# Four edits at the starts of three stages of a two-block transformer kernel on one core: input products in step with the shift on ScalarE, a first chunk split on GpSimd, raw gates copied out, post norm sums on TensorE

## The chip, the core and the metric

The kernel runs on one core of one Trainium2 chip. The core has TensorE (PE, matrix products out of SBUF into eight PSUM banks), VectorE (DVE), ScalarE (ACT), GpSimd (POOL) and SyncE (SP, which issues the DMAs). Each engine runs its own list of instructions in order, and they meet by semaphores. The metric is the time of one execution on the device in microseconds; lower is better.

## The reference, cut to what matters

Two blocks follow each other on x of 512 tokens by 1024 features, all in float32. Of the first block:

```python
h = rms_norm(x, mix_pre_norm) * (1 + sc_m) + sh_m
proj = h @ w_in                      # cq, ckv, index keys, then the inputs of the RWKV group
...
x = x + g_m * rms_norm(mix, mix_post_norm)
hf = rms_norm(x, ffn_pre_norm) * (1 + sc_f) + sh_f
f = (silu(hf @ w_ffn_gate) * (hf @ w_ffn_up)) @ w_ffn_down
x = x + g_f * rms_norm(f, ffn_post_norm)
```

The second block begins with

```python
h = h + 0.5 * swiglu(rms_norm_2(h, norm_ffn[0, 0]), ffn_w_gate, ffn_w_up, ffn_w_down)
```

## The kernel before, in words

The activations stand transposed in SBUF: `x` and `h` are eight tiles of 128 features by 512 tokens. A product of float32 matrices is made of three products of rounded numbers: each operand is split into a high part (a rounding copy by ScalarE) and a low part (the operand less its high part, by VectorE), and TensorE adds high x high, high x low and low x high. Weights stream from HBM in chunks of 1 MB (eight rows of 128 by 256 columns) through a ring of four slots; `Split.high` and `Split.low` split each chunk into `wt_hi` and `wt_lo`, of which there are two each. Chunks are loaded by SyncE as soon as the chunk four before is split (`low_done`). The order of the instructions on each engine is the order in which the code is written; nothing reorders them.

Three stages are touched.

**inproj**, the input products (`in_proj_stage`, by way of `linear_part`). The first chunk, in_q, gives two output tiles, in_kv one, then twelve of in_rkv. Before, `normed_vector` makes each of the eight features in two instructions on VectorE, times gain and norm (L713, the norm's value standing in a bank) and plus the shift (L716). ScalarE copies the high part; the low part of even tiles is VectorE's (L720), of odd ones GpSimd's (L748). The chunk is split whole (L521, L536), and `product3` runs through the eight features for output tile 0, then again for tile 1. Between in_kv and in_rkv stands `ik_product`, the product of the index keys, a plain float32 product of `h` itself (L814): it is the first to need the tiles of `h`.

**ffn1** (`ffn_part` with `mix`). The stage begins with two norms at once (`MixNorm`): VectorE forms five small columns (`new_squares`, L435 to L443, 128x4 in `coef`), ScalarE takes the root, VectorE the inverse, and TensorE spreads both norms over banks 5 and 7 (L428). Then VectorE updates each tile k in three instructions (L458: h times coefficient and norm; L460: x plus h; L464: the next norm), and the low part is the fourth (L471). The first chunk is split in four quarters, by ScalarE (L548) and VectorE (L564), between these. `first_chunks` makes TensorE go through the features once, for the two gate tiles and, three features behind, the two up tiles.

**ffn2** (`ffn_part` with `post`), behind ffn1 in the same section. ffn1's output f lies in `h`. `PostNorm` needs its column sums of squares: six tiles are summed by GpSimd while ffn1 ends (into `acc`, named mcq in the trace), the last two are squared by ScalarE and added by VectorE (L299), and TensorE sums the one tile over its partitions (L308). Root, inverse and spread (L318, L322, L312) follow, then for each tile VectorE's two instructions of `update` (L328 into a bank, L330 from it into x) and the low part (L674); ScalarE makes the high part (L653) and the square (L654), and GpSimd adds the squares for the next norm (L740). That norm is applied late (`defer`): gates and ups are products of the un-normed features, and VectorE multiplies them by the inverse root `rs` (L691, L697, L703), gates before SiLU (L1271). A product into the gate banks 0 and 1 waits until the gates in them are scaled (`s_gate`).

## Time and profile before

| what | value |
| --- | --- |
| median of 3 runs | 2852.81 us (2852.09 to 2854.67) |
| the profiled execution | 2850.93 us |
| its span | 2849.1 us |
| TensorE busy | 2718.7 us, 95% of the span |
| VectorE busy | 1318.2 us, 46% |
| ScalarE busy | 845.7 us, 30% |
| GpSimd busy | 550.8 us, 19% |
| mean granted clock of TensorE | 0.975 |

The profile is one execution as the hardware recorded it. Its span runs from the first to the last instruction; the time of the execution is a little longer. Busy is the sum over an engine's instructions. The granted clock is a share of TensorE's full speed, 2.4 GHz, and has two levels, so 0.5 is 1.2 GHz. Names on the left of `<-` are written, those on the right read; `bank` is PSUM, all others are SBUF or, with `in_`, HBM.

### The profile page before, as it was taken

How to read it: one execution, taken by the hardware profiler on the slowest of the kernel's cores; microseconds unless marked ns; L12 is line 12 of the kernel's file. 1: busy time of each engine (PE TensorE's matmuls, PEld its weight loads, DVE VectorE, ACT ScalarE, POOL GpSimd, SP SyncE). 2: the span in 40 equal slices, each digit the busy share in tenths (PEclk: the TensorE clock that was granted, in tenths of full speed). 3: DMA queues.
4: the chain of work that ended last, by engine and by line, in shares of the span. 5: the costliest groups of instructions: out<-in, count | busy, mean ns of one | idle time of the engine just before them, and what ended most of it. 6: DMA issues, size and time to landing. Idle time of an engine off the chain costs nothing. (4 is left out here: it accounts for less than half of the span.)

```text
span 2849.1 us, 39056 instructions
## 1 busy us (share of the span) xinstructions
PE 2718.7 (95%) x16402; PEld 2167.3 (76%) x16402; DVE 1318.2 (46%) x1862; ACT 845.7 (30%) x1264; POOL 550.8 (19%) x379
## 2 busy tenths in 40 slices
PE   6989898989999899999989999999999999999998
PEld 4768764778888688887858888888888746788886
DVE  3464668553333633435455434353333556543433
ACT  3231235531212422123253212132222346421212
POOL 2000113412112230212301202123021100031202
PEclk8999989989999899999999999999999999999999
DMA  8250310123232223323203232233232230233221
GB/s 262 62 177 4 121 37 4 60 74 104 89 104 79 84 95 98 104 78 105 89 1 116 92 103 89 89 104 104 89 104 80 62 104 1 89 104 103 89 93 41
DMA packets 256943, 248.26 MB, mean 87 GB/s; under 512 B 25972, under 2 KB 252088, under 8 KB 256640
## 3 DMA queue, kind: packets, MB, share of 16 engines
q1 hardware_dynamic: 256562, 245.70, 27.6%
q8 instruction: 130, 2.13, 0.3%
q14 instruction: 45, 0.37, 0.0%
q10 hardware_dynamic: 206, 0.06, 0.0%
HBM read 241.52 MB, written 2.12 MB: 86 GB/s over the span
## 5 line engine op out<-in xcount | busy, mean ns | idle before, releaser
L536 DVE TENSOR_TENSOR dense_wt_lo<-ring,dense_wt_hi 128x2048 fp32r<-128x2048 f32 (+1 forms) x177 | 437.6, 2472 | 291.1 <-ACT dense_wt_hi L521 291.1
L521 ACT CAST dense_wt_hi<-ring 128x2048 fp32r<-128x2048 f32 (+1 forms) x177 | 328.1, 1854 | 764.6 <-PE bank L796 752.8
L1292 POOL TENSOR_TENSOR dense_act_hi<-dense_act,const 128x512 fp32r<-128x512 f32 x110 | 214.8, 1952 | 1326.7 <-DVE dense_act L1284 1326.7
L796 PE MATMUL bank<-feat_hi,dense_wt_hi 128*128 128x512 f32 x1344 | 416.0, 391 | 2.9 <-DVE dense_silu L1271 2.9
L796 PE MATMUL bank<-feat_lo,dense_wt_hi 128*128 128x512 f32 x1344 | 414.9, 390 | 0.0
L796 PE MATMUL bank<-feat_hi,dense_wt_lo 128*128 128x512 f32 x1344 | 414.8, 390 | 0.0
L796 PEld LDWEIGHTS bank<-feat_hi,dense_wt_hi 128*128 128x128 f32 x1344 | 253.0, 188 | 56.6 <-issue 4.3
L796 PEld LDWEIGHTS bank<-feat_lo,dense_wt_hi 128*128 128x128 f32 x1344 | 253.0, 188 | 52.7
L796 PEld LDWEIGHTS bank<-feat_hi,dense_wt_lo 128*128 128x128 f32 x1344 | 252.9, 188 | 52.6
L796 PE MATMUL bank<-dense_act_hi,dense_wt_hi 128*128 128x512 f32 x912 | 282.3, 391 | 6.4 <-DVE dense_act_lo L604 5.5
L796 PE MATMUL bank<-dense_act_hi,dense_wt_lo 128*128 128x512 f32 x912 | 281.5, 390 | 0.0
L796 PE MATMUL bank<-dense_act_lo,dense_wt_hi 128*128 128x512 f32 x912 | 281.4, 390 | 0.0
L796 PEld LDWEIGHTS bank<-dense_act_hi,dense_wt_hi 128*128 128x128 f32 x912 | 171.2, 188 | 44.1 <-DVE dense_wt_lo L601 5.9
L796 PEld LDWEIGHTS bank<-dense_act_lo,dense_wt_hi 128*128 128x128 f32 x912 | 171.5, 188 | 35.8
L796 PEld LDWEIGHTS bank<-dense_act_hi,dense_wt_lo 128*128 128x128 f32 x912 | 171.5, 188 | 35.7
L1284 DVE TENSOR_TENSOR dense_act<-dense_silu,bank 128x512 f32<-128x512 f32 x110 | 70.7, 684 | 259.7 <-PE bank L796 258.7
L1262 DVE SCALAR_TENSOR_TENSOR x<-bank,x 128x512 f32<-128x512 f32 x96 | 61.8, 686 | 234.2 <-PE bank L796 234.2
L1215 ACT ACTIVATE dense_silu<-dense_silu 128x512 f32<-128x512 f32 x88 | 54.1, 632 | 390.9 <-DVE dense_silu L1271 390.9
L1271 DVE TENSOR_TENSOR dense_silu<-bank,rs 128x512 f32<-128x512 f32 x88 | 56.7, 686 | 230.3 <-PE bank L796 229.7
L1294 POOL TENSOR_TENSOR dense_act_lo<-dense_act,dense_act_hi 128x512 fp32r<-128x512 f32 x110 | 150.6, 1369 | 16.5 <-issue 1.3
L272 POOL TENSOR_TENSOR h<-h 128x512 f32<-128x512 f32 x30 | 39.2, 1305 | 409.7 <-ACT h L257 408.6
L796 PE MATMUL bank<-last_feat_hi,dense_wt_hi 128*128 128x512 f32 x352 | 108.9, 390 | 0.0
(619 smaller groups left out, 3787.3 us busy)
## 6 DMA issues: line engine op xcount, KB each, us to landing
ring<-in_ffn_w_gate SPq DMA_DIRECT2D x44, 1024.0 KB, 5.3
ring<-in_ffn_w_up SPq DMA_DIRECT2D x44, 1024.0 KB, 5.3
ring<-in_ffn_w_down SPq DMA_DIRECT2D x32, 1024.0 KB, 5.1
ring<-in_ada_w SPq DMA_DIRECT2D x24, 1024.0 KB, 7.5
ring<-in_ffn_w_down SPq DMA_DIRECT2D x16, 768.0 KB, 4.4
...
```

The source lines that it names most:

```text
L272: K.nc.gpsimd.tensor_tensor(K.h[:, 0, :], K.h[:, 0, :], K.h[:, k, :], ALU.add)
L521: self.nc.scalar.copy(self.wh[:, n % 2, 0:words], K.ring[:, n % RING, 0:words]).then_inc(K.high_done, 1)
L536: self.nc.vector.tensor_tensor(self.wl[:, n % 2, 0:words], K.ring[:, n % RING, 0:words], self.wh[:, n % 2, 0:words].bitcast(F32), ALU.subt ...
L796: lasts[m] = pe.matmul(outs[m], a, b, start=n == 0 and p == 0, stop=end and p == 2)
L1215: nc.scalar.activation(g[:, m, :], g[:, m, :], ACT.Silu).then_inc(s_silu, 1)
L1262: v.scalar_tensor_tensor(to, bank, 0.5, to, ALU.mult, ALU.add).then_inc(s_free, 1)
L1271: v.tensor_tensor(g[:, m, :], K.bank[m][:, :], K.rs[:, :], ALU.mult).then_inc(s_gate, 1)
L1284: v.tensor_tensor(a[:, m, :], g[:, m, :], K.bank[2 + m][:, :], ALU.mult).then_inc(s_act, 1)
L1292: nc.gpsimd.tensor_tensor(ah[:, f, :], a[:, i % 2, :], K.k("ones")[:, 0:1].broadcast_to([P, T]), ALU.mult)
L1294: nc.gpsimd.tensor_tensor(al[:, f, :], a[:, i % 2, :], ah[:, f, :].bitcast(F32), ALU.subtract).then_inc(s_al, 1)
```

## The change

Four edits, each at one of the three stages.

1. *inproj.* It gets a `NormedSource` and takes the path that three other stages had (`source_scalar`, `source_vector`): ScalarE and VectorE split the first chunk in quarters between the features, and TensorE makes the two tiles of in_q in step, six products for each feature. A feature is made by one instruction of VectorE (gain and norm); ScalarE adds the shift as it makes the high part, VectorE as it makes the low one, for all eight tiles. Since `ik_product` needs the whole `h`, GpSimd adds the shift in place once the low part of that tile is out, and TensorE waits for all eight before `ik_product`. That GpSimd makes no low parts any more is part of it.
2. *ffn1.* The four quarters of the first chunk are subtracted by GpSimd (`mix_pool`) in place of VectorE, and VectorE waits for them before it splits chunk 1.
3. *ffn2, the gates.* ScalarE copies the two raw gate tiles of the first chunk from their banks into the SiLU tile; the product of chunk 2 waits for these copies in place of the scaled gates, and VectorE scales the copies.
4. *ffn2, the post norm.* The two last squares are summed by TensorE into the same columns as the tile of sums, so that VectorE's two additions go. And in VectorE's loop the low part of tile k-1 now stands between the two instructions of tile k.

```diff
-    def add(self, dve):
-        v = self.K.nc.vector
-        for m in range(2):
-            dve.wait_ge(self.s_sq, m + 1)
-            ins = v.tensor_tensor(self.acc, self.acc, self.sq[m], ALU.add)
-            if m == 0:
-                dve.drain()
-        ins.then_inc(self.s_add, 1)
-
-    def sums(self, pe):
+    def sums(self, pe, prev):
+
         K = self.K
-        pe.wait_ge(self.s_add, 1)
-        for b in range(TB):
-            last = pe.matmul(K.bank[6][:, b:b + 1], self.acc[:, b * P:(b + 1) * P], K.k("ones")[:, 0:1], start=True, stop=True)
+        pe.wait_ge(prev.s_acc, 1)
+        pe.wait_ge(prev.done[0], prev.done[1] - 2)
+        for m, x in enumerate([self.acc] + list(self.sq)):
+            if m:
+                pe.wait_ge(self.s_sq, m)
+            for b in range(TB):
+                last = pe.matmul(K.bank[4][:, b:b + 1], x[:, b * P:(b + 1) * P], K.k("ones")[:, 0:1], start=m == b == 0, stop=m == 2 and b == TB - 1)
         last.then_inc(self.s_sum, 1)
         pe.wait_ge(self.s_inv, 1)
...
-    def update(self, dve, k):
-        K, v = self.K, self.K.nc.vector
+    def scale(self, dve, k):
+        K = self.K
         if k == 0:
             dve.wait_ge(self.s_spread, 1)
-        v.scalar_tensor_tensor(K.bank[4 + 2 * (k % 2)][:, :], K.h[:, k, :], self.coef(k), K.bank[5][:, :], ALU.mult, ALU.mult)
+        K.nc.vector.scalar_tensor_tensor(K.bank[4 + 2 * (k % 2)][:, :], K.h[:, k, :], self.coef(k), K.bank[5][:, :], ALU.mult, ALU.mult)
         dve.drain()
-        v.tensor_tensor(K.x[:, k, :], K.bank[4 + 2 * (k % 2)][:, :], K.x[:, k, :], ALU.add).then_inc(self.s_x, 1)
+
+    def add(self, k):
+        K = self.K
+        K.nc.vector.tensor_tensor(K.x[:, k, :], K.bank[4 + 2 * (k % 2)][:, :], K.x[:, k, :], ALU.add).then_inc(self.s_x, 1)
...
-        K, v = self.K, self.nc.vector
+    def mix_pool(self, pool):
+        K = self.K
         n = self.pieces
-        self.mix.new_squares(dve)
         for j in range(4):
             part = slice(2 * j * WC, 2 * (j + 1) * WC)
-            dve.wait_ge(self.s_wh, j + 1)
-            v.tensor_tensor(self.wl[:, n % 2, part], K.ring[:, n % RING, part], self.wh[:, n % 2, part].bitcast(F32),
-                            ALU.subtract).then_inc(self.s_wl, 1)
-            if j == 1:
-                self.mix.inverse(dve)
-        dve.drain().then_inc(K.low_done, 1)
+            pool.wait_ge(self.s_wh, j + 1)
+            self.nc.gpsimd.tensor_tensor(self.wl[:, n % 2, part], K.ring[:, n % RING, part], self.wh[:, n % 2, part].bitcast(F32),
+                                         ALU.subtract).then_inc(self.s_wl, 1)
+        pool.drain().then_inc(K.low_done, 1)
+
+    def mix_vector(self, dve, name):
+        K = self.K
+        self.mix.new_squares(dve)
+        self.mix.inverse(dve)
         for k in range(KD + 1):
             if k < KD:
                 self.mix.update(dve, k)
@@ -573,6 +568,7 @@
                 dve.wait_ge(self.s_hh, k)
                 self.mix.low(self.hl[:, k - 1, :], self.hh[:, k - 1, :], k - 1).then_inc(self.s_hl, 1)
             if k == 2:
+                dve.wait_ge(K.low_done, K.plan.segments[name]["split0"] + 1)
                 self.low(dve, name, 1)
...
-            if source.ready(k):
-                act.wait_ge(*source.ready(k))
-            c(self.hh[:, k, :], source.tile(k)).then_inc(self.s_hh, 1)
+            source.high(act, k, self.hh[:, k, :]).then_inc(self.s_hh, 1)
         act.drain().then_inc(K.high_done, 1)
 
     def source_vector(self, dve):
         K, source, v = self.K, self.source, self.nc.vector
         n = self.pieces
+        source.make(dve, source.order[0])
         for at, k in enumerate(source.order):
             if at % 2 == 0:
                 part = slice(k * WC, (k + 2) * WC)
                 dve.wait_ge(self.s_wh, at // 2 + 1)
                 v.tensor_tensor(self.wl[:, n % 2, part], K.ring[:, n % RING, part], self.wh[:, n % 2, part].bitcast(F32),
                                 ALU.subtract).then_inc(self.s_wl, 1)
+            if at + 1 < KD:
+                source.make(dve, source.order[at + 1])
             dve.wait_ge(self.s_hh, at + 1)
-            v.tensor_tensor(self.hl[:, k, :], source.tile(k), self.hh[:, k, :].bitcast(F32), ALU.subtract).then_inc(self.s_hl, 1)
+            source.low(k, self.hl[:, k, :], self.hh[:, k, :].bitcast(F32)).then_inc(self.s_hl, 1)
         dve.drain().then_inc(K.low_done, 1)
...
             for k in range(KD + 1):
                 if k < KD:
-                    self.post.update(dve, k)
+                    self.post.scale(dve, k)
                 if k:
                     dve.wait_ge(self.s_hh, k)
                     v.scalar_tensor_tensor(self.hl[:, k - 1, :], K.x[:, k - 1, :], self.defer(k - 1), self.hh[:, k - 1, :].bitcast(F32),
                                            ALU.mult, ALU.subtract).then_inc(self.s_hl2 if k % 2 == 0 else self.s_hl, 1)
+                if k < KD:
+                    self.post.add(k)
...
-    def normed_vector(self, dve):
-
-        K, v = self.K, self.nc.vector
-        gain, shift = self.norm
-        if self.rstd:
-            dve.wait_ge(self.rstd.s_out, 1)
-        for k in range(KD):
-            ins = v.scalar_tensor_tensor(K.h[:, k, :], K.x[:, k, :], gain(k), self.value, ALU.mult, ALU.mult)
...
-                ins = v.tensor_scalar(K.h[:, k, :], K.h[:, k, :], shift(k), None, ALU.add)
...
     def features_vector(self, dve, first_low, name=None):
-        self.first_low = first_low
-        if self.norm:
-            return self.normed_vector(dve)
         if self.defer:
             if not self.prev:
                 first_low(dve)
@@ -741,11 +703,9 @@
                 if k < KD - 1:
                     pool.drain()
             ins.then_inc(self.s_add, 1)
-        if not self.norm:
-            return
-        for k in range(1, KD, 2):
-            pool.wait_ge(self.s_hh, k + 1)
-            self.nc.gpsimd.tensor_tensor(self.hl[:, k, :], K.h[:, k, :], self.hh[:, k, :].bitcast(F32), ALU.subtract).then_inc(self.s_hl2, 1)
+        if self.mix:
+            self.mix_pool(pool)
...
-                    if i >= 2:
+                    if post and c == 2:
+                        pe.wait_ge(s_raw, 2)
+                    elif i >= 2:
...
                 if c == 0:
+                    for m in range(2 if post else 0):
+                        act.wait_ge(K.tiles_done, plan.tile(name, c, m))
+                        nc.scalar.copy(g[:, m, :], K.bank[m][:, :]).then_inc(s_raw, 1)
...
-                        dve.wait_ge(K.tiles_done, plan.tile(name, c, m))
-                        v.tensor_tensor(g[:, m, :], K.bank[m][:, :], K.rs[:, :], ALU.mult).then_inc(s_gate, 1)
+                        if post and c == 0:
+                            dve.wait_ge(s_raw, m + 1)
+                        else:
+                            dve.wait_ge(K.tiles_done, plan.tile(name, c, m))
+                        v.tensor_tensor(g[:, m, :], g[:, m, :] if post and c == 0 else K.bank[m][:, :], K.rs[:, :], ALU.mult).then_inc(s_gate, 1)
...
-            if source and j == 0:
+            if source and (seg, j) == chunks[0][:2]:
...
+    def high(self, act, k, dst):
+        if self.ready(k):
+            act.wait_ge(*self.ready(k))
+        return self.nc.scalar.copy(dst, self.tile(k))
+
+    def low(self, k, dst, high):
+        return self.nc.vector.tensor_tensor(dst, self.tile(k), high, ALU.subtract)
+
+
+class NormedSource:
+
+    order, front, shift = range(KD), None, 0
+
+    def __init__(self, K, gain, bias, value):
+        self.K, self.gain, self.bias, self.value = K, gain, bias, value
+
+    def begin(self, st):
+        self.s_h, self.s_whole = st.sems("normed", "shifted")
+
+    def make(self, dve, k):
+        K = self.K
+        K.nc.vector.scalar_tensor_tensor(K.h[:, k, :], K.x[:, k, :], self.gain(k), self.value, ALU.mult, ALU.mult).then_inc(self.s_h, 1)
+
+    def high(self, act, k, dst):
+        act.wait_ge(self.s_h, k + 1)
+        return self.K.nc.scalar.activation(dst, self.K.h[:, k, :], ACT.Identity, bias=self.bias(k))
+
+    def low(self, k, dst, high):
+        return self.K.nc.vector.scalar_tensor_tensor(dst, self.K.h[:, k, :], self.bias(k), high, ALU.add, ALU.subtract)
+
+    def whole(self, pool, s_hl):
+        K = self.K
+        for k in range(KD):
+            pool.wait_ge(s_hl, k + 1)
+            K.nc.gpsimd.tensor_scalar(K.h[:, k, :], K.h[:, k, :], self.bias(k), None, ALU.add).then_inc(self.s_whole, 1)
...
         pe.wait_ge(box["wik_in"], 16)
+        pe.wait_ge(source.s_whole, KD)
         product(pe, K.bank[6][0:72, :], [(box["wik"][:, k, :], K.h[:, k, :]) for k in range(KD)]).then_inc(box["ik_pe"], 1)
...
-    def causal(pool):
+    def on_pool(pool):
+        source.whole(pool, box["split"].s_hl)
         pool.wait_ge(box["scored"], 1)
...
+    source = NormedSource(K, *norm, K.norm_value)
     linear_stage(K, "inproj", tiles, banks=6, scalar=lambda t: False,
```

The places where the order moves, as lists of instructions. GpSimd in inproj, from the start of the stage (`branch`) to its end, before and after:

```order
L886 UNCONDITIONAL_BRANCH
L748 TENSOR_TENSOR inproj__feat_lo<-h,inproj__feat_hi 128x512 [waits inproj__feat_high] x4
L1728 ISA [waits inproj__scored]
L1728 AFFINE_SELECT y<-y 128x128
L865 UNCONDITIONAL_BRANCH
```

```order
L846 UNCONDITIONAL_BRANCH
L1497 ISA
L1497 TENSOR_SCALAR h<-h,mod 128x512 [waits inproj__feat_low_even] x8
L1738 AFFINE_SELECT y<-y 128x128 [waits inproj__scored]
L825 UNCONDITIONAL_BRANCH
```

Four subtractions that waited for high parts give way to eight additions in place that wait for low parts; the selection on the scores stays behind them.

VectorE in inproj, from its first instruction in the stage, before and after, both up to feature 3:

```order
L713 SCALAR_TENSOR_TENSOR h<-x,coef,bank 128x512
L716 TENSOR_SCALAR h<-h,mod 128x512
L713 SCALAR_TENSOR_TENSOR h<-x,coef,bank 128x512
L716 TENSOR_SCALAR h<-h,mod 128x512
L720 TENSOR_TENSOR inproj__feat_lo<-h,inproj__feat_hi 128x512 [waits inproj__feat_high]
L536 TENSOR_TENSOR inproj_wt_lo<-ring,inproj_wt_hi 128x2048 [waits high_done]
L713 SCALAR_TENSOR_TENSOR h<-x,coef,bank 128x512
L716 TENSOR_SCALAR h<-h,mod 128x512
L713 SCALAR_TENSOR_TENSOR h<-x,coef,bank 128x512
L716 TENSOR_SCALAR h<-h,mod 128x512
```

```order
L1484 SCALAR_TENSOR_TENSOR h<-x,coef,bank 128x512
L596 TENSOR_TENSOR inproj_wt_lo<-ring,inproj_wt_hi 128x512 [waits inproj__first_high]
L1484 SCALAR_TENSOR_TENSOR h<-x,coef,bank 128x512
L1491 SCALAR_TENSOR_TENSOR inproj__feat_lo<-h,mod,inproj__feat_hi 128x512 [waits inproj__feat_high]
L1484 SCALAR_TENSOR_TENSOR h<-x,coef,bank 128x512
L1491 SCALAR_TENSOR_TENSOR inproj__feat_lo<-h,mod,inproj__feat_hi 128x512 [waits inproj__feat_high]
L596 TENSOR_TENSOR inproj_wt_lo<-ring,inproj_wt_hi 128x512 [waits inproj__first_high]
L1484 SCALAR_TENSOR_TENSOR h<-x,coef,bank 128x512
L1491 SCALAR_TENSOR_TENSOR inproj__feat_lo<-h,mod,inproj__feat_hi 128x512 [waits inproj__feat_high]
```

The shift (L716) is gone from VectorE, the split of the chunk stands in quarters between the features, and each feature is made one ahead of the low half before it.

VectorE at the start of ffn1, the columns of the two norms and the first update, before and after:

```order
L435 TENSOR_TENSOR coef<-bank,coef 128x4
L437 SCALAR_TENSOR_TENSOR coef<-bank,coef 128x4
L439 TENSOR_TENSOR coef<-coef 128x4
L441 TENSOR_TENSOR coef<-coef 128x4
L443 TENSOR_SCALAR coef<-coef 128x4
L564 TENSOR_TENSOR dense_wt_lo<-ring,dense_wt_hi 128x512 x2
L452 RECIPROCAL coef<-coef 128x4
L564 TENSOR_TENSOR dense_wt_lo<-ring,dense_wt_hi 128x512 x2
L458 SCALAR_TENSOR_TENSOR h<-h,coef,bank 128x512
```

```order
L434 TENSOR_TENSOR coef<-bank,coef 128x4
L436 SCALAR_TENSOR_TENSOR coef<-bank,coef 128x4
L438 TENSOR_TENSOR coef<-coef 128x4
L440 TENSOR_TENSOR coef<-coef 128x4
L442 TENSOR_SCALAR coef<-coef 128x4
L451 RECIPROCAL coef<-coef 128x4
L457 SCALAR_TENSOR_TENSOR h<-h,coef,bank 128x512
L459 TENSOR_TENSOR x<-x,h 128x512
```

The four subtractions around the inverse (L452, now L451) are gone; GpSimd has them.

VectorE at the start of ffn2, from the inverse of the post norm, before and after:

```order
L322 RECIPROCAL ffn_post_col<-ffn_post_col 128x4
L536 TENSOR_TENSOR dense_wt_lo<-ring,dense_wt_hi 128x2048
L328 SCALAR_TENSOR_TENSOR bank<-h,coef,bank 128x512
L330 TENSOR_TENSOR x<-bank,x 128x512
L328 SCALAR_TENSOR_TENSOR bank<-h,coef,bank 128x512
L330 TENSOR_TENSOR x<-bank,x 128x512
L674 SCALAR_TENSOR_TENSOR feat_lo<-x,par,feat_hi 128x512
L328 SCALAR_TENSOR_TENSOR bank<-h,coef,bank 128x512
L330 TENSOR_TENSOR x<-bank,x 128x512
```

```order
L318 RECIPROCAL ffn_post_col<-ffn_post_col 128x4
L529 TENSOR_TENSOR dense_wt_lo<-ring,dense_wt_hi 128x2048
L324 SCALAR_TENSOR_TENSOR bank<-h,coef,bank 128x512
L329 TENSOR_TENSOR x<-bank,x 128x512
L324 SCALAR_TENSOR_TENSOR bank<-h,coef,bank 128x512
L657 SCALAR_TENSOR_TENSOR feat_lo<-x,par,feat_hi 128x512
L329 TENSOR_TENSOR x<-bank,x 128x512
L324 SCALAR_TENSOR_TENSOR bank<-h,coef,bank 128x512
L657 SCALAR_TENSOR_TENSOR feat_lo<-x,par,feat_hi 128x512
```

The low part of tile k-1 moved from behind to ahead of the addition of tile k.

ScalarE in ffn2, from the square of the last tile, before and after:

```order
L654 ACTIVATE h<-x 128x512
L521 CAST dense_wt_hi<-ring 128x2048
L697 ACTIVATE rs<-bank,const 128x512
L1215 ACT_TABLE_LOAD
L1215 ACTIVATE dense_silu<-dense_silu 128x512 x2
L521 CAST dense_wt_hi<-ring 128x2048
L1215 ACTIVATE dense_silu<-dense_silu 128x512 x2
```

```order
L637 ACTIVATE h<-x 128x512
L1167 COPY dense_silu<-bank 128x512 x2
L514 CAST dense_wt_hi<-ring 128x2048
L682 ACTIVATE rs<-bank,const 128x512
L1180 ACT_TABLE_LOAD
L1180 ACTIVATE dense_silu<-dense_silu 128x512 x2
L514 CAST dense_wt_hi<-ring 128x2048
L1180 ACTIVATE dense_silu<-dense_silu 128x512 x2
```

Two copies of banks into the SiLU tile now stand ahead of the cast of chunk 2 and of the root.

## Rows read from the trace of the kernel before

**Rows 1.** Waits of TensorE: us in all, times, longest.

```profile
PE bank L806 <- DVE feat_lo L471: 8.3, 2, 4.9
...
PE bank L806 <- DVE feat_lo L674: 4.6, 2, 3.8
```

**Rows 2.** Timeline, input products: start us, us, instruction [idle before, releaser].

```profile
43.99 0.75 DVE L713 SCALAR_TENSOR_TENSOR h<-x,coef,bank 128x512 f32<-128x512 f32 x1 [0.32 <-PEq L1027]
...
49.41 0.79 PE L780 MATMUL bank<-inproj__feat_hi,inproj_wt_hi 128*128 128x512 f32 x1 [6.19 <-DVE inproj_wt_lo L536]
...
73.01 7.03 PE L814 MATMUL bank<-h,y 128*72 128x512 f32 x16
```

**Rows 3.** Timeline, VectorE and GpSimd; two lines' kinds: least, median, longest ns.

```profile
47.06 2.29 DVE L536 TENSOR_TENSOR inproj_wt_lo<-ring,inproj_wt_hi 128x2048 fp32r<-128x2048 f32 x1
...
47.26 3.23 POOL L748 TENSOR_TENSOR inproj__feat_lo<-h,inproj__feat_hi 128x512 fp32r<-128x512 f32 x1 [12.49 <-ACT inproj__feat_hi L647]
...
963.79 1.28 POOL L740 TENSOR_TENSOR h<-h 128x512 f32<-128x512 f32 x1 [14.98 <-ACT h L654]
...
964.44 1.18 DVE L674 SCALAR_TENSOR_TENSOR feat_lo<-x,par,feat_hi 128x512 fp32r<-128x512 f32 x1
...
L674 DVE SCALAR_TENSOR_TENSOR feat_lo<-x,par,feat_hi x8: 743/749/1193, 962.4 to 977.1; 128x512 fp32r<-128x512 f32 x8
...
L2639 POOL TENSOR_SCALAR abin__acc<-abin__acc x4: 1491/2419/3592, 1349.2 to 1374.2; 128x512 f32<-128x512 f32 x4
```

**Rows 4.** Timeline, start of ffn1.

```profile
575.75 1.14 ACT L548 CAST dense_wt_hi<-ring 128x512 fp32r<-128x512 f32 x2 [2.11 <-PEq L865]
...
576.45 0.16 DVE L441 TENSOR_TENSOR coef<-coef 128x4 f32<-128x4 f32 x1
...
576.77 1.28 DVE L564 TENSOR_TENSOR dense_wt_lo<-ring,dense_wt_hi 128x512 fp32r<-128x512 f32 x2
...
576.89 0.30 ACT L448 ACTIVATE coef<-coef,const 128x4 f32<-128x4 f32 x1
...
578.20 2.07 PE L428 MATMUL bank<-const,coef 128*128 128x128 f32 x8 [0.40 <-DVE coef L452]
...
579.81 0.75 DVE L458 SCALAR_TENSOR_TENSOR h<-h,coef,bank 128x512 f32<-128x512 f32 x1 [0.49 <-issue]
...
585.20 1.19 PE L806 MATMUL bank<-feat_hi,dense_wt_hi 128*128 128x512 f32 x2 [4.93 <-DVE feat_lo L471]
```

**Rows 5.** Timeline, start of ffn2.

```profile
954.65 1.88 ACT L521 CAST dense_wt_hi<-ring 128x2048 fp32r<-128x2048 f32 x1
...
956.84 0.26 ACT L318 ACTIVATE ffn_post_col<-bank,const 128x4 f32<-128x4 f32 x1 [0.31 <-PE bank L308]
...
960.92 0.75 DVE L328 SCALAR_TENSOR_TENSOR bank<-h,coef,bank 128x512 f32<-128x512 f32 x1
...
970.31 0.73 PE L806 MATMUL bank<-feat_hi,dense_wt_hi 128*128 128x512 f32 x2 [0.84 <-DVE feat_lo L674]
...
974.81 0.74 DVE L328 SCALAR_TENSOR_TENSOR bank<-h,coef,bank 128x512 f32<-128x512 f32 x1
```

**Rows 6.** Timeline, ffn2 behind its first two chunks.

```profile
982.23 0.62 PE L806 MATMUL bank<-feat_hi,dense_wt_lo 128*128 128x512 f32 x2
...
982.68 0.62 PE L806 MATMUL bank<-feat_hi,dense_wt_hi 128*128 128x512 f32 x2
...
982.94 1.91 ACT L521 CAST dense_wt_hi<-ring 128x2048 fp32r<-128x2048 f32 x1 [5.33 <-PE bank L806]
...
987.18 3.35 DVE L703 RECIPROCAL rs<-rs 128x512 f32<-128x512 f32 x1
...
992.12 1.19 PE L796 MATMUL bank<-feat_hi,dense_wt_hi 128*128 128x512 f32 x2 [2.93 <-DVE dense_silu L1271]
```

**Rows 7.** Window: us, busy of five engines, clock, DMA; group of the page: busy, mean.

```profile
992.20:998.20 6.00, 6.00 (x15) 4.76 (x16) 5.12 (x5) 2.22 (x2) 3.86 (x2) 0.52 0.00 0
...
L1215 ACT ACTIVATE dense_silu<-dense_silu 128x512 f32<-128x512 f32 x88 | 54.1, 632 | 390.9 <-DVE dense_silu L1271 390.9
```

80 lines of the change are left out of this document (27 added, 53 removed).

## The prediction, made before the changed kernel had run

> **What bounds the kernel now.** I read the page first: TensorE is busy for 95% of the span (the table above), so an edit gains only where TensorE stands still or runs at the lower of its two clocks. The chain that ended last is no help here, being put down mostly to issue. The waits of TensorE and the timeline around them name the places, and the change works at four of them. TensorE stands 4.9 and 3.4 us (8.3 together) for `feat_lo` at the start of ffn1 and 4.6 us for `feat_lo` at the start of ffn2 [rows 1], 6.2 us before the input products [rows 2], and 2.9 us for `dense_silu` in ffn2 [rows 6]. In the input products TensorE starts at 49.41, 5.4 us after VectorE's first instruction, and reaches the product of the index keys at 73.01 [rows 2]. At both ffn starts it is VectorE that paces the first features [rows 4, 5]. Everywhere between, TensorE is dense, so I take a shift at one of these places as carried whole to the end.
>
> **A port that two edits meet.** Edits 1 and 2 both give GpSimd work while VectorE sets the pace, so I read how the two run together [rows 3]. GpSimd's subtraction that started at 47.26, just behind VectorE's 2.29 us one, took 3.23 us; its instruction at 963.79, with nothing ahead, 1.28. The other way round VectorE's `feat_lo` at 964.44, begun under that GpSimd instruction, took 1.18 us, where the least of its kind is 0.743. GpSimd's one kind of TENSOR_SCALAR took 1.49 us at the least and 3.59 at the most. So one engine waits for the other's whole instruction when both read SBUF with two tiles in play.
>
> The Trainium skill ("SBUF — State Buffer", "Who interferes with whom") says more: a VectorE instruction with two SBUF inputs contends with any GpSimd instruction that reads SBUF, and the first to issue keeps the pair to its end. The 3.23 and 1.18 agree; that VectorE waits for a GpSimd TENSOR_SCALAR no row here shows. By the page edit 1 gains next to nothing; without it, the 7 us that are worked out below. It speaks against edits 1 and 2.
>
> **Edit 1, input products.** *Without the port:* VectorE makes feature 0 at 43.99 (0.75 us, and the next instruction starts some 0.66 behind), splits a quarter of the chunk (0.64, half of the x2 of 1.28 [rows 4]), makes feature 1 and takes the low half of 0, so TensorE starts near 46.8, 2.6 us earlier. A feature then costs VectorE 0.66 + 0.66 + 0.64/2 = 1.64 us. TensorE's six products of it take 2.55 us at the lower clock (0.425 each, 14 in the 6.0 us of [rows 7]) and 1.36 at the higher (0.2265 each: two start 0.45 behind two [rows 6]). With some 16 products at the lower clock the two tiles end near 60.4 and in_kv's 24 products near 65.9, where before the key product started at 73.0: 7 us gained.
> *With the port:* GpSimd adds the shift to tile k once low k is out, eight times 1.49 us. Each falls under VectorE's making of the next feature, which reads a bank, and the next low half, with two SBUF inputs, waits for its end. Two features cost 0.64 (quarter) + 2 x (1.49 + 0.66) = 4.9 us, less the overlap of one instruction's end with the next; I step 4.7 to 5.1. Low 0 ends at 46.6, low 1 at 48.9, low 3 at 54.0, low 5 at 59.1, low 7 at 64.2. GpSimd's last addition then starts at once (64.3 to 65.8), ahead of VectorE's split of in_kv, half as wide as the 2.29 us one (1.4). in_kv's products run 67.3 to 72.8: 0.2 us gained. Of the ends I take 0.2, since the operations are those of [rows 3] but for one operand. ScalarE's shift and casts lie under VectorE. The ring's next load is issued some 15 us later (the first split is complete at 64.3, not 49.4), but its chunk is the fifth of the stage, a 5 us transfer with 30 us before it is cast: hidden.
>
> **Edit 2, GpSimd splits ffn1's first chunk.** It takes four subtractions of 0.64 us off VectorE, which hold the update of feature 0 to 579.81 [rows 4]. *Left alone* VectorE could update at 577.9, when the first spread (2.07 us from 575.75) is out; the second spread behind it ends at 579.9, where the step that needs it came 1.6 us after 579.81: 1.5 us gained. *With the port:* GpSimd's first quarter starts at 576.4, when the first of ScalarE's two casts is out, and the product of two `coef` columns at 576.45 has two SBUF inputs. It waits to 577.7. The next small instruction may wait for the second quarter, to 579.1; then come the root (0.30), the inverse, the second spread to 582.0, and the sum x+h under the third quarter. TensorE's first product starts at 586.1 in place of 585.20: 0.9 us lost. If the small instruction, with one input, doesn't wait, the same steps gain 0.25. I take 0.9 lost, since both waits are for whole instructions as in [rows 3]; bounds: 1.5 gained, 1.5 lost.
>
> **Edit 4 and the new order of the post norm, ffn2.** Two additions go from VectorE and 16 small products come to TensorE, most of them under ScalarE's squares. ScalarE's cast (954.65, 1.88 us) holds the root to 956.55; before, the root waited 0.31 us longer, to 956.84 [rows 5]: 0.3 us gained. Then VectorE's loop. Before, a feature's step comes every (974.81 - 960.92)/6 = 2.32 us [rows 5], of which about 2.1 are three instructions and the rest the port: GpSimd's sum of squares meets every second low half (0.743 against 1.19 [rows 3]). In the new order the low half comes before the addition, which reads a bank, and 0.6 us before the square that starts GpSimd; the two stop meeting, and a step takes about 2.15. Feature 1's step starts at 960.62, feature 4's at 967.07, and low 3, 0.83 behind it, is out at 968.7; TensorE waits for it until 970.31 now and is dense behind it. 1.6 us gained in all; at the least 0.3, the root alone, should the higher clock come later.
>
> **Edit 3, raw gates copied out.** Before, TensorE ends the first two chunks near 989.2 and waits for gates scaled by the inverse (3.35 us from 987.18) to 992.12 [rows 6]: 2.9 us. After that idle time the granted clock is 0.52 for 6.0 us, in which 14 products take 0.425 each instead of 0.2265 [rows 7]: 2.8 us. Now ScalarE copies the gates (2 x 0.63, as its activations of this size [rows 7]) before the cast of chunk 2, which started at 982.94. Counted with the 1.6 above: copies 981.3 to 982.6, cast (1.9) to 984.5, VectorE's split (2.29) to 986.8; TensorE ends at 987.6 and goes on at once, at the full clock. The inverse runs from 986.8, the activations come at 994.2, chunk 3's split at 997, and TensorE wants it at 998.5. Gained: 2.9 + 2.8 = 5.7 us. The cover is thin, 0.8 us at chunk 2 and 1.5 at chunk 3; if it goes, some 3 us are left.
>
> **The sum.** -0.2 + 0.9 - 1.6 - 5.7 = -6.6 us. The profiled execution took 2850.93 (span 2849.1 and 1.8 around it), so 2844.3; the median of the runs lies 1.9 above it. I say **2846 us**.
>
> **The rivals.**
> *The port doesn't bind in the input products* (the addition of a column isn't held, or doesn't hold VectorE): 7 us instead of 0.2, so 2839. For it: no row shows VectorE waiting for a TENSOR_SCALAR. Against: GpSimd's own was stretched to 3.59 [rows 3]. Chance 0.15.
> *The gates' cover is gone:* chunk 2's split comes late behind copies and cast, TensorE waits two us and the clock falls all the same. 5.7 shrinks to 2 or 3: 2849. Against: 0.8 us of slack. Chance 0.15.
> *Slower, GpSimd's additions are slow.* The key product waits for all eight, and each holds VectorE, so each us more of an addition's own time moves in_kv by 8. To lose the 6.4 us of the other terms and 0.2% more takes 12.1 us: an addition of 1.49 + 12.1/8 = 3.0 us or more. The stretched ones took up to 3.59, but 2.1 of that was VectorE's. At 3.3 us it is 2860. Chance 0.07.
> *As forecast:* 0.63, own range 2842 to 2849.
>
> **Range and chances.** 2838 to 2851 takes in the first two rivals and the bounds of edit 2, and leaves out the third. A measurement tells about 0.2%, 5.7 us, from no change: below 2847.1 is faster. Of the forecast's 0.63 I put 0.43 below that, 0.19 within and 0.01 above; the first rival is faster; of the second 0.01 is faster and 0.14 within. Faster 0.59, same 0.33, slower 0.08.
>
> **What would show it.** Input products: TensorE starts at 46.8, GpSimd has eight TENSOR_SCALARs on `h` of 1.5 us or stretched, VectorE low halves of up to 1.4 us, and the key product starts near 72.8. ffn1: a small `coef` row of over 1 us, TensorE's first product 0.9 us later against the stage's start. ffn2: steps of 2.15 us, no wait for `dense_silu`, granted clock 1.00 there. Wrong it would be if the key product starts near 66, if the clock stays low through the first two tiles, or if TensorE still stops behind ffn2's second chunk.

## The result and the profile after

| | before | after |
|---|---|---|
| median of the runs, us | 2853.02 (2852.09 to 2854.67, 4 runs) | 2836.01 (2835.05 to 2841.01, 4 runs) |
| ratio of after to before | | 0.9944, 95% interval 0.9932 to 0.9956 |
| profiled execution, us (its span) | 2850.93 (2849.1) | 2836.70 (2834.8) |

The change takes about 16 us off where 6.6 were forecast, and the median lies 2 us below the range. A second, later comparison of the same two kernels gave 0.9949 (0.9937 to 0.9961), which is 14.5 us.

The timeline of the input products after the change, the counterpart of [rows 2]:

```profile
43.13 0.75 DVE L1484 SCALAR_TENSOR_TENSOR h<-x,coef,bank 128x512 f32<-128x512 f32 x1 [0.32 <-PEq L987]
...
45.06 0.75 DVE L1491 SCALAR_TENSOR_TENSOR inproj__feat_lo<-h,mod,inproj__feat_hi 128x512 fp32r<-128x512 f32 x1
...
45.91 12.86 POOL L1497 TENSOR_SCALAR h<-h,mod 128x512 f32<-128x512 f32 x8 [11.78 <-DVE inproj__feat_lo L1491]
45.95 1.19 PE L756 MATMUL bank<-inproj__feat_hi,inproj_wt_hi 128*128 128x512 f32 x2 [3.60 <-DVE inproj__feat_lo L1491]
...
46.38 0.76 DVE L1491 SCALAR_TENSOR_TENSOR inproj__feat_lo<-h,mod,inproj__feat_hi 128x512 fp32r<-128x512 f32 x1
...
54.83 2.06 DVE L1491 SCALAR_TENSOR_TENSOR inproj__feat_lo<-h,mod,inproj__feat_hi 128x512 fp32r<-128x512 f32 x2
...
57.34 1.63 DVE L529 TENSOR_TENSOR inproj_wt_lo<-ring,inproj_wt_hi 128x1024 fp32r<-128x1024 f32 x1
...
65.27 7.03 PE L774 MATMUL bank<-h,y 128*72 128x512 f32 x16
```

The three kinds by their own lines (least, median and longest ns; first and last start):

```profile
L1491 DVE SCALAR_TENSOR_TENSOR inproj__feat_lo<-h,mod,inproj__feat_hi x8: 735/742/1191, 45.1 to 55.7; 128x512 fp32r<-128x512 f32 x8
L1497 POOL TENSOR_SCALAR h<-h,mod x8: 1562/1572/1726, 45.9 to 57.2; 128x512 f32<-128x512 f32 x8
L657 DVE SCALAR_TENSOR_TENSOR feat_lo<-x,par,feat_hi x8: 750/752/754, 953.9 to 968.9; 128x512 fp32r<-128x512 f32 x8
```

GpSimd adds eight times without a gap and VectorE's low halves under it take 0.74 us at the median; only the last is late (1.19), and the split behind it (1.63). When a low half starts in GpSimd's addition matters. Two of them, one that was not held and the one that was, beside GpSimd's addition of that moment:

```profile
49.16 1.56 POOL L1497 TENSOR_SCALAR h<-h,mod 128x512 f32<-128x512 f32 x1
49.65 0.74 DVE L1491 SCALAR_TENSOR_TENSOR inproj__feat_lo<-h,mod,inproj__feat_hi 128x512 fp32r<-128x512 f32 x1
...
55.66 1.56 POOL L1497 TENSOR_SCALAR h<-h,mod 128x512 f32<-128x512 f32 x1
55.70 1.19 DVE L1491 SCALAR_TENSOR_TENSOR inproj__feat_lo<-h,mod,inproj__feat_hi 128x512 fp32r<-128x512 f32 x1
```

The first starts 0.49 us into the addition, the second 0.04. The key product starts at 65.27, not at the 72.8 of the forecast. The third line of the kinds is ffn2's: no low half is held there any more, as predicted.

ffn1, against [rows 4]:

```profile
568.53 0.16 DVE L434 TENSOR_TENSOR coef<-bank,coef 128x4 f32<-128x4 f32 x1 [3.22 <-PEq L825]
...
569.50 0.17 DVE L442 TENSOR_SCALAR coef<-coef 128x4 f32<-128x4 f32 x1
569.65 5.40 POOL L556 TENSOR_TENSOR dense_wt_lo<-ring,dense_wt_hi 128x512 fp32r<-128x512 f32 x4 [8.07 <-ACT dense_wt_hi L541]
...
571.44 1.25 DVE L459 TENSOR_TENSOR x<-x,h 128x512 f32<-128x512 f32 x1
...
574.25 1.35 DVE L459 TENSOR_TENSOR x<-x,h 128x512 f32<-128x512 f32 x1
...
577.23 1.19 PE L766 MATMUL bank<-feat_hi,dense_wt_hi 128*128 128x512 f32 x2 [4.88 <-DVE feat_lo L470]
```

VectorE's five small columns are over within 0.02 us of the start of GpSimd's first subtraction (569.50 and 0.17 against 569.65), and none took longer than 0.17 us. Two additions to `x`, least 0.69 us, take 1.25 and 1.35 under the subtractions.

ffn2, against [rows 5, 6] (timeline, then windows with the busy time of TensorE, its granted clock and the DMA share):

```profile
949.03 0.25 ACT L314 ACTIVATE ffn_post_col<-bank,const 128x4 f32<-128x4 f32 x1
...
978.79 3.35 DVE L688 RECIPROCAL rs<-rs 128x512 f32<-128x512 f32 x1
...
979.58 0.62 PE L766 MATMUL bank<-feat_hi,dense_wt_lo 128*128 128x512 f32 x2
980.03 0.61 PE L756 MATMUL bank<-feat_hi,dense_wt_hi 128*128 128x512 f32 x2
```

```profile
974.00:980.00 6.00, 6.00 (x26) 1.00 0.00 1
980.00:986.00 6.00, 6.00 (x28) 1.00 0.56 176
```

TensorE passes from chunk 1 to chunk 2 at 980.03 without a gap and at 2.4 GHz, while the inverse is still being computed (978.79 to 982.14).

### The profile page after: what moved, and what is told of

Its sections match the earlier page's. It is cut to its first block and busy times, and to the rows that moved or that the text cites. A ratio compares the mean times of both kernels' runs of the same rounds, so it can differ in the third digit from the quotient of the medians.

```text
span 2834.8 us, 39099 instructions
## 1 busy us (share of the span) xinstructions
PE 2716.3 (96%) x16418; PEld 2170.8 (77%) x16418; DVE 1312.3 (46%) x1855; ACT 848.4 (30%) x1269; POOL 563.6 (20%) x387
```

## Where the time went, stage by stage

The gain of the whole is only a few times the uncertainty of a ratio, so I cut each trace at five marks: A, VectorE's TENSOR_TENSOR on `mod` that ends the start stage; B, the index-key product; C, the first `coef` instruction of ffn1; D, the last pair of `h<-bank,h` in ffn1; E, the third pair of `dense_act` in ffn2. The row of D and E of each trace, of before and then of after:

```profile
952.79 1.29 DVE L1266 TENSOR_TENSOR h<-bank,h 128x512 f32<-128x512 f32 x2 [1.83 <-PE bank L796]
...
1038.44 1.28 DVE L1284 TENSOR_TENSOR dense_act<-dense_silu,bank 128x512 f32<-128x512 f32 x2 [4.80 <-PE bank L796]
```

```profile
945.38 1.29 DVE L1230 TENSOR_TENSOR h<-bank,h 128x512 f32<-128x512 f32 x2 [1.83 <-PE bank L756]
...
1023.52 1.28 DVE L1251 TENSOR_TENSOR dense_act<-dense_silu,bank 128x512 f32<-128x512 f32 x2 [4.79 <-PE bank L756]
```

Stretches in us, with the variants of the next section:

| | A to B: edit 1 | B to C: no edit | C to D: edit 2 | D to E: edits 3, 4 | E to the end: no edit |
|---|---|---|---|---|---|
| before | 29.75 | 502.7 | 377.1 | 85.65 | 1810.7 |
| after | 22.88 | 503.3 | 376.9 | 78.14 | 1811.3 |
| the change again | 22.46 | 504.9 | 376.1 | 78.04 | 1810.1 |
| `only_edit1` | 22.21 | 506.5 | 376.2 | 85.16 | 1809.9 |
| `no_edit2` | 22.21 | 507.0 | 377.8 | 78.00 | 1806.8 |
| `no_edit3` | 22.22 | 504.1 | 377.0 | 83.01 | 1809.9 |
| `no_edit4` | 22.22 | 505.6 | 377.7 | 79.66 | 1812.2 |

Between before and after, edit 1's stretch gives 6.9 us and that of edits 3 and 4 gives 7.5, 14.4 in all; A itself came 0.9 us earlier, with nothing changed ahead of it. Stretches whose code is the same move by up to 5 us from trace to trace, so single traces are compared below only within a short stretch.

Part of that movement can be placed. Behind the key product, `only_edit1`, `no_edit3` and `no_edit4` lose 1.5 us against the other traces within the same 17 us. Eight of those microseconds, 14 to 22 behind the key product, with the change and then in `no_edit4` (TensorE's products in brackets, its granted clock after the five engines):

```profile
79.27:87.27 8.00, 8.00 (x40) 6.81 (x40) 0.47 (x3) 0.57 (x3) 0.00 (x0) 0.79 0.00 0
```

```profile
78.75:86.75 8.00, 8.00 (x34) 6.94 (x34) 0.47 (x3) 0.57 (x3) 0.00 (x0) 0.57 0.00 0
```

TensorE is busy throughout in both, and the one with the lower granted clock, 0.57 against 0.79, gets 34 products done and not 40. Before the change it was 0.79 as well. In ffn1 the scatter arises at the stage's start: the first `dense_act` comes 38.3 to 40.2 us behind C in every trace but the two `ffn1` versions below, and from there to the last one it is 305.2 us in all of them.

## Experiments

### Each edit by itself: `only_edit1`, `no_edit2`, `no_edit3`, `no_edit4`

`only_edit1` is the changed kernel with the three undoings below together (of edit 4 both its sums and its order):

```diff
 # no_edit2: in mix_pool's place, VectorE between new_squares and its loop
+        for j in range(4):
+            dve.wait_ge(self.s_wh, j + 1)
+            K.nc.vector.tensor_tensor(self.wl[:, n % 2, part], K.ring[:, n % RING, part], ...)
+            if j == 1:
+                self.mix.inverse(dve)
 # no_edit3: gates straight from the banks
-                        nc.scalar.copy(g[:, m, :], K.bank[m][:, :]).then_inc(s_raw, 1)
-                        v.tensor_tensor(g[:, m, :], g[:, m, :] if post and c == 0 else K.bank[m][:, :], K.rs[:, :], ALU.mult)
+                        v.tensor_tensor(g[:, m, :], K.bank[m][:, :], K.rs[:, :], ALU.mult)
 # no_edit4: PostNorm and its call of before (VectorE adds the squares; scale and add together, then low)
-                    self.post.scale(dve, k)
+                    self.post.update(dve, k)
-                    self.post.add(k)
```

Expected of `only_edit1`: 

> Edit 1 alone, the three other edits undone. Theory A (the port does not hold VectorE's low halves under GpSimd's additions of a column): the index-key product starts 6.9 us earlier, its start stage set aside, and the kernel takes 6.9 us less than before, a ratio near 0.9976. Theory B (my forecast's port binds, and the trace of the change owes its early key product to something else in it): 0.2 us less, a ratio of 0.9999, with low halves of up to 1.4 us.

Measured: 2844.25 us, ratio 0.9972 (0.9958 to 0.9986), 8 us less (4 to 12); A to B is 22.21, 7.5 us less. Theory A holds: edit 1 alone gives some 7 us. Whether B to C gives a part of it back can't be said: it is 503.3 to 507.0 in the table's traces with edit 1, but there is only one trace without it (502.7).

Expected of `no_edit2`: 

> The change with edit 2 undone: VectorE splits ffn1's first chunk. Read from the trace: TensorE's first product in ffn1 against VectorE's start of that stage. With the change it stands 8.70 us behind it (568.53 to 577.23), before 9.45. Theory A (edit 2 helps a little, since only the two-tile updates are held by GpSimd): 9.4 to 9.5 here, and later products catch up most of it, so the whole run is within 1 us of the change. Theory B (edit 2 as forecast, 0.9 us of loss by the port): 8.5 or less here.

Measured: 2836.99 us (one run); the first product stands 9.13 us behind the stage's first VectorE instruction (9.13 in `only_edit1` too, 9.48 before, 8.70 with edit 2). So edit 2 starts TensorE 0.4 to 0.8 us earlier, and C to D does not show it: 376.1 to 377.7 in the table's four traces with edit 2, 376.2 to 377.8 in the three without. This is nearer to theory A, though its 9.4 was not reached: a small help at the start, and at the end no effect that stands out from a spread of 1.6 us.

Expected of `no_edit3`: 

> The change with edit 3 undone: VectorE scales the gates from the banks again, behind the inverse. Theory A (edit 3 gives its wait of 2.9 and its clock of 2.8): 5.7 us more than the change, some 2842, with a wait of 2.5 to 3.5 us for the gates in ffn2 and a granted clock of about 0.5 for 6 us behind it. Theory B (the reordered post norm alone already moved the inverse early enough, or the clock does not fall): less than 3 us more.

Measured: 2843.07 us, ratio to before 0.9968 (0.9957 to 0.9979), so 5 to 7 us more than the change by its two ratios. The timeline and the windows:

```profile
986.08 0.70 PE L756 MATMUL bank<-feat_hi,dense_wt_hi 128*128 128x512 f32 x2 [2.93 <-DVE dense_silu L1230]
```

```profile
980.00:986.00 6.00, 3.15 (x13) 1.00 0.56 175
986.00:992.00 6.00, 5.92 (x19) 0.72 0.01 3
```

D to E is 83.01 in place of 78.04 to 78.14: 4.9 us. The wait is back (2.93), and behind it the granted clock was 0.72 for six microseconds, where before it had been 0.52. In `only_edit1`, which waits 2.93 us too, it was 0.72 over 989.00:995.00. Theory A, with a smaller share of the clock: 4.9 less 2.9 leaves 2.0 us, not 2.8.

Expected of `no_edit4`: 

> The change with the post norm's sums and its loop's order undone. Read from the trace: root to root of ffn2 against the end of ffn1, and the step of a feature. Theory A (as forecast): a step of 2.32 us instead of 2.15 and the root 0.3 us later, so 1.3 to 1.6 us more in ffn2's first chunks, if TensorE waits for them. Theory B (the order gives nothing, only the root does): 0.3 to 0.5 us more, a step of 2.15 here too.

Measured: 2841.76 us in one run, a figure that B to C and E to the end blur. D to E is 79.66: 1.5 to 1.6 us more. The root stands 4.05 us behind D (948.07 to 952.12) and 3.65 with the change, a feature's step takes 2.31 us (956.12 to 970.00 for six) and 2.15 with the change, and low halves are held again, to 1.19 us:

```profile
L662 DVE SCALAR_TENSOR_TENSOR feat_lo<-x,par,feat_hi x8: 743/754/1189, 957.5 to 972.3; 128x512 fp32r<-128x512 f32 x8
```

Theory A.

### The disputed pairs alone: `pairs`

```diff
+            for n in range(16):   # VectorE, one of five kinds
+                v.scalar_tensor_tensor(vo[:, n * 512:(n + 1) * 512], va[:, 0:512], vcol[:, 0:1], vb[:, 0:512], ALU.add, ALU.subtract)
+            for n in range(6):    # GpSimd at the same time, one of three kinds
+                nc.gpsimd.tensor_scalar(gt[:, n * 512:(n + 1) * 512], gt[:, n * 512:(n + 1) * 512], gcol[:, 0:1], None, ALU.add)
```

Expected: 

> The disputed pairs by themselves: nothing of the reference is computed (the output is a scaled piece of x). In each of 18 blocks GpSimd issues six instructions of 128x512 (an addition of a column, or a product with a number, or an addition of two tiles) while VectorE issues nothing, 16 instructions of 128x512 with two SBUF inputs (with a column between, or without one), 4 of 128x2048 with two SBUF inputs, 16 with a bank, or 16 with one tile; five blocks more have VectorE alone. Theory A (what counts is the form of GpSimd's instruction: only one with two tile inputs excludes a VectorE instruction with two): under the column and the number VectorE's stay within 0.1 us of their time alone; under two tiles they are held, and GpSimd's are stretched by up to one VectorE instruction. Theory B (a part of each GpSimd instruction excludes, about its first 0.45 us): every GpSimd form holds VectorE a bit, 0.3 to 0.5 us for each of GpSimd's, and the one of 2.29 us stretches all three forms to 3 us and more. Theory C (column against number): the product with a number is stretched and the addition of a column is not.

Measured, of VectorE's two-input instruction alone, and under GpSimd's column addition, its product with a number and its addition of two tiles (least, median, longest ns); then GpSimd's column addition and its addition of two tiles, each with VectorE idle:

```profile
L3052 DVE SCALAR_TENSOR_TENSOR vo<-va,vcol,vb x16: 747/748/752, 10.0 to 20.0; 128x512 f32<-128x512 f32 x16
L3074 DVE SCALAR_TENSOR_TENSOR vo<-va,vcol,vb x16: 739/739/1180, 66.4 to 78.9; 128x512 f32<-128x512 f32 x16
L3096 DVE SCALAR_TENSOR_TENSOR vo<-va,vcol,vb x16: 739/740/1095, 141.4 to 153.4; 128x512 f32<-128x512 f32 x16
L3118 DVE SCALAR_TENSOR_TENSOR vo<-va,vcol,vb x16: 739/740/1749, 209.4 to 225.4; 128x512 f32<-128x512 f32 x16
L3151 POOL TENSOR_SCALAR gt<-gt,gcol x6: 1564/1564/1571, 57.0 to 64.7; 128x512 f32<-128x512 f32 x6
L3199 POOL TENSOR_TENSOR gt<-gt,gu x6: 1262/1262/1262, 201.9 to 208.0; 128x512 f32<-128x512 f32 x6
```

And under the addition of two tiles: VectorE's 2.29 us split and its instruction with a bank, then GpSimd beside that split:

```profile
L3126 DVE TENSOR_TENSOR vo<-va,vb x4: 3344/3346/3398, 242.5 to 252.4; 128x2048 f32<-128x2048 f32 x4
L3130 DVE SCALAR_TENSOR_TENSOR vo<-va,vcol,bank x16: 740/740/746, 258.1 to 268.0; 128x512 f32<-128x512 f32 x16
L3211 POOL TENSOR_TENSOR gt<-gt,gu x6: 1256/3306/3309, 242.5 to 256.8; 128x512 f32<-128x512 f32 x6
```

GpSimd's column addition and its product with a number, each beside the 2.29 us split:

```profile
L3163 POOL TENSOR_SCALAR gt<-gt,gcol x6: 1557/1558/5724, 93.2 to 108.3; 128x512 f32<-128x512 f32 x6
L3187 POOL TENSOR_SCALAR gt<-gt x6: 1484/2642/2648, 166.7 to 178.6; 128x512 f32<-128x512 f32 x6
```

How long the longest VectorE instruction took beyond its time alone, us:

| VectorE | alone | under column | under number | under two tiles |
|---|---|---|---|---|
| two SBUF inputs and a column, 512 | 0.75 | +0.43 | +0.35 | +1.00 |
| two SBUF inputs, 512 | 0.69 | +0.41 | +0.46 | +1.11 |
| two SBUF inputs, 2048 | 2.29 | +0.41 | +0.46 | +1.11 |
| one SBUF input and a bank, 512 | 0.74 | 0 | 0 | 0 |
| one SBUF input (TENSOR_SCALAR), 512 | 0.48 | +0.42 | +0.40 | +1.05 |

Theory B's core holds: every form of GpSimd's holds VectorE, and only for a part of its time. A column addition of 1.56 us holds it for 0.43 at most; an addition of two tiles (1.26) holds it for nearly its whole length. Two of B's figures miss: it gave two tiles no more than 0.5 us, and it had all three forms stretched to 3 us and more, where the product with a number took 2.65. A falls by the column and the number, which hold VectorE 0.35 us and more, and C by the column, which is stretched. The other way round GpSimd does wait for a whole instruction of VectorE's (1.26 became 3.31 beside the 2.29 us split), and its column addition of 1.56 us waited through two of them (5.72).

### GpSimd's shift with two tile operands: `whole_two`

```diff
-            K.nc.gpsimd.tensor_scalar(K.h[:, k, :], K.h[:, k, :], self.bias(k), None, ALU.add)
+            K.nc.gpsimd.tensor_tensor(K.h[:, k, :], K.h[:, k, :], self.bias(k).broadcast_to([P, T]), ALU.add)
```

Expected: 

> The change, with GpSimd's eight additions of the shift written as additions of two tile operands (the column spread along the row). Theory A (two tile inputs exclude each other, as my forecast had it for all forms): VectorE's low halves take 1.0 to 1.4 us, two features cost 4.3 to 5.1 us instead of 3.25, and the index-key product starts 27 to 29.5 us behind the first instruction on mod, where the change has 22.9; the kernel is 4 to 6.5 us slower than the change. Theory B (the low halves merely fall beside the exclusive part of GpSimd's instruction): 22 to 24 us, no slower than 1 us.

Measured: 2839.48 us, ratio to before 0.9946 (0.993 to 0.9963). A to B is 23.97. VectorE's low halves:

```profile
L1491 DVE SCALAR_TENSOR_TENSOR inproj__feat_lo<-h,mod,inproj__feat_hi x8: 746/866/1092, 46.6 to 58.5; 128x512 fp32r<-128x512 f32 x8
```

Two features cost 3.72 us instead of 3.25, and A to B grows by 1.1 to 1.8 us. So even this form does little. The first low half beside it:

```profile
47.46 1.04 POOL L1497 TENSOR_TENSOR h<-h,mod 128x512 f32<-128x512 f32 x1 [11.49 <-DVE inproj__feat_lo L1491]
...
47.95 1.09 DVE L1491 SCALAR_TENSOR_TENSOR inproj__feat_lo<-h,mod,inproj__feat_hi 128x512 fp32r<-128x512 f32 x1
```

The low half starts 0.49 us into GpSimd's instruction, behind VectorE's instruction with a bank, and is held 0.35 us more (1.09 against 0.74). Counting 0.74 back from its end, it got its way at 48.30, 0.2 us before GpSimd's ended at 48.50. It is much the same under two tiles: 0.19 us in [rows 3] (964.88 against 965.07) and 0.13 to 0.19 in the pairs. Under a column addition it is 1.07 us (56.15 against 57.22 in the change, 1.0 to 1.1 in the pairs). So the spread column holds VectorE as a second tile does, and most of the hold falls beside the instruction with a bank. Theory A's 4 to 6.5 us is about four times too much; theory B's 22 to 24 us from A to B is met, and its reason in part, since VectorE is still held 0.35 us.

### Twice the additions: `whole_double`

```diff
+        pool.drain()
+        for k in range(KD):
+            K.nc.gpsimd.tensor_scalar(K.h[:, k, :], K.h[:, k, :], K.k("eps")[:, 2:3], None, ALU.add).then_inc(self.s_whole, 1)
```

Expected: 

> The change with 16 column additions of GpSimd instead of 8 (the second pass adds a column of zeros). The rival in which GpSimd's additions set the key product: eight take 12.9 us and end 6.5 us before TensorE wants them, so eight more end 6.4 us too late. Theory A: the key product starts 29 us behind the first instruction on mod, up from 22.9, and TensorE stands some 6 us for shifted rows. Theory B (the additions run faster when VectorE is no longer in its loop, or the product is asked for later): 3 us or less.

Measured: 2853.46 us; A to B is 31.81, 9 us more:

```profile
59.99 15.12 POOL L1500 TENSOR_SCALAR h<-h,const 128x512 f32<-128x512 f32 x8 [0.17 <-issue]
...
75.26 9.07 PE L774 MATMUL bank<-h,y 128*72 128x512 f32 x16 [9.33 <-POOL h L1500]
```

TensorE stands 9.33 us for GpSimd, and the product itself then takes 9.07 us at a mean granted clock of 0.78, where it took 7.03 after no such wait. Theory A's wait, and more: the second eight additions took 15.12 us, where the first eight of the change took 12.86. GpSimd's eight end at 58.8 in the change and are wanted at 65.3; with twice as many all that the change gave is gone (one run).

### A column in the ab stage: `abin_column`

```diff
-            nc.gpsimd.tensor_scalar(acc[:, (g + 1) % 2, PAD:], cur[:, PAD:], 1.0 / (2 << g), None, ALU.mult)
+            nc.gpsimd.tensor_scalar(acc[:, (g + 1) % 2, PAD:], cur[:, PAD:], K.k("ones")[:, g:g + 1], None, ALU.mult)
```

Expected: 

> The change, with the four products with a number that GpSimd runs in the ab stage read as products with a column of ones (this leaves out the scale 1/2 to 1/16 of the window sums). Theory C (a number is stretched, a column is not): all four take 1.5 to 1.7 us, where 1.49, 2.4 and 3.5 were seen. Theory B (the place in time decides, beside VectorE's 2.29 us splits): one or two of them still take over 2.4 us.

Measured (2839.64 us):

```profile
L2650 POOL TENSOR_SCALAR abin__acc<-abin__acc,const x4: 1567/2494/3413, 1338.5 to 1363.8; 128x512 f32<-128x512 f32 x4
```

Two of the four took 3.41 us, the two that ran beside VectorE's splits; the other two took 1.57. The column is stretched as the number was: theory B, the place decides.

### The lesson tried in ffn1: `ffn1_bank`, `ffn1_pipe`, `change_again`

```diff
 # ffn1_bank (update of MixNorm)
-        v.scalar_tensor_tensor(K.h[:, k, :], K.h[:, k, :], self.coef(k), K.bank[5][:, :], ALU.mult, ALU.mult)
+        v.scalar_tensor_tensor(bank, K.h[:, k, :], self.coef(k), K.bank[5][:, :], ALU.mult, ALU.mult)
-        v.tensor_tensor(K.x[:, k, :], K.x[:, k, :], K.h[:, k, :], ALU.add)
+        v.tensor_tensor(K.x[:, k, :], bank, K.x[:, k, :], ALU.add)
 # ffn1_pipe, on top (VectorE's loop)
+            self.mix.normed(dve, k)
+            self.mix.added(k + 1)
+            self.mix.scaled(dve, k + 2)
+            dve.wait_ge(self.s_hh, k + 1)
+            self.mix.low(self.hl[:, k, :], self.hh[:, k, :], k).then_inc(self.s_hl, 1)
+            dve.drain()
```

Expected of `ffn1_bank`: 

> The change, with ffn1's update writing h times its inverse to a bank, as the post norm of ffn2 does, so that the addition to x has one SBUF input where it had two. The pair table says that an instruction with a bank is never held. Theory A (edit 2's late additions, 1.25 and 1.35 us instead of 0.69, are the port): both take 0.69, TensorE's first product stands 7.4 to 7.7 us behind the stage's first VectorE instruction instead of 8.70, and GpSimd's four subtractions take 1.26 each. Whole time: at most 1.2 us less than the change, since what TensorE gets early here it gave back before; not to be told from no change. Theory B (the late additions wait for something else): 8.6 to 8.8 again.

Measured: 2839.98 us, ratio 0.9952 (0.994 to 0.9965); the first product 7.66 us behind the stage's start, and no addition held:

```profile
L460 DVE TENSOR_TENSOR x<-bank,x x8: 692/692/693, 576.6 to 599.1; 128x512 f32<-128x512 f32 x8
```

Theory A: edit 2's late additions were the port, since the same additions with one SBUF input are not held. C to D is 375.1.

Expected of `ffn1_pipe`: 

> The same, and VectorE's loop of ffn1 in an order with one drain a feature instead of two (norm k, add k+1, scale k+2, low k). A step is 2.9 us now (0.82 + 0.77 + 0.67 + 0.66); with one drain about 2.75. Theory A (VectorE paces ffn1's first chunks): 1 to 2.5 us less than the change in all, ratio to before near 0.994 to 0.9935. Theory B (the lower clock of TensorE in these chunks gives it back, as it did for edit 2): the first product 0.7 to 1.3 us earlier, ffn1 as long as now.

Measured: 2838.0 us, ratio 0.9948 (0.9935 to 0.9962); first product at 7.16 us, C to D 373.3, 2.8 us less than the shortest with the change. The first `dense_act` comes 35.5 us behind C (37.3 in `ffn1_bank`), where all the others have 38.3 to 40.2. Theory A by the stretch, in one trace; the whole time can't tell it from the change.

Expected of `change_again`: 

> The change once more, as it is, for two things. How far do stages that no edit touches move from run to run: the stretch from the index-key product to ffn1 took 503.3 us with the change and 502.7 before, but 504 to 508 in the variants, whose code is the same there. And the ratio: 0.9944 was measured; sum of the stages' own differences is 15 us, which would be 0.9947.

Measured: 2839.38 us, ratio 0.9949 (0.9937 to 0.9961). B to C is 504.9 us. So the forecast of this ratio from the stages was right, and neither ffn1 version is shown to beat the change.

## Why the prediction was wrong, and where it was right

- **Edit 1, "with the port": the step that failed.** Forecast 0.2 us, measured 6.9 to 7.5. I took from [rows 3] that "one engine waits for the other's whole instruction". That is true of GpSimd behind VectorE (the 3.23 us there), not of VectorE behind a TENSOR_SCALAR of GpSimd: 0.43 us of 1.56. Two features cost 3.3 us (first low half 45.06, third 48.33), not 4.9. Where the low halves fell was luck on top: those that were not held start 0.47 us or later in GpSimd's addition, just behind the hold, and only the last, 0.04 in, pays. Were all seven of them held, they would have cost, by my estimate, 7 x 0.43 = 3.0 us of the 7. The 1.18 us row was a subtraction of two tiles, whose hold is nearly the whole (0.65 into it and 0.44 more, of 1.28); I carried it over to a form with one tile. And the 3.59 of [rows 3] was GpSimd's wait, which says nothing of VectorE's.
- **Edit 1, "without the port"** was right almost to the digit: TensorE's start was worked out as 46.8 and came at 45.95 behind a start stage 0.87 shorter; the key product was to come near 66, with 7 us gained. The first rival, with 0.15, is what happened (VectorE was held only once). Its "for" was that no row showed VectorE waiting for a TENSOR_SCALAR; that deserved more weight than a rule extended from other forms.
- **The Trainium skill's rule** ("SBUF — State Buffer", "Who interferes with whom"): two SBUF inputs of VectorE contend with a GpSimd read. The pairs agree that they contend and that an instruction with one SBUF input and a bank does not (0.74 us in all four cases). They differ from its rule that the first to issue keeps the pair to its end: VectorE was held 0.43 us by an instruction of 1.56.
- **Edit 2.** Forecast 0.9 us lost. The first product came 0.4 to 0.8 us earlier, and at the stage's end no effect can be told. Failed: that GpSimd meets the small `coef` instructions. It starts 1.12 us behind VectorE's first instruction of the stage, not 0.68 (576.4 against 575.72), when the five columns are made. What it meets are two additions to `x` (+0.56 and +0.66); `ffn1_bank` showed that.
- **Edit 4.** Forecast 1.6, measured 1.5 to 1.6 beside edit 3. Root 0.4 earlier (0.3 forecast), step 2.15, no low half held: as written. Without edit 3 it gave 2.2 to 2.6 (`no_edit3` against `only_edit1` and before), why it gave more there isn't shown.
- **Edit 3.** Forecast 5.7, measured 4.9. The wait of 2.9 is right; the clock's share was 2.0 in `no_edit3`, while 2.8 stood in the one trace of before. Without edit 4 it gave 5.5 to 6.0 (`no_edit4` against `only_edit1` and before); the two edits together were forecast at 7.3 and gave 7.5. TensorE asked for chunk 2 1.2 us behind its split (0.8 forecast), so the cover held.
- **The slower rival** rests on the step that failed, since it lets each addition hold VectorE to its end. What `whole_double` shows of it is another path to the same loss: a late key product costs TensorE its wait in full and the clock behind it. That needed 6.5 us more of GpSimd than it has.
- **The range** took each rival and bound by itself. The first rival's 2839 with edit 2 at its bound of 1.5 gained in place of 0.9 lost is 2836.8, already outside of 2838. Also, "everywhere between, TensorE is dense" was too much: in the trace of before it stands 7.69 us ahead of its product at 463.2, and behind B the granted clock moved a stretch by 1.5 us.

Summed by stages the change gives 14.4 us, and 16 and 14.5 by the two ratios. For 1.5 of the 5 us by which stretches that no edit touches move, the granted clock goes with it (above); what sets it, and where the rest comes from, is open.
